# Differential attention: the transposition of the probabilities one slot later, from a buffer pair of their own

## Chip, cores and metric

One NeuronCore of a Trainium2 chip runs the whole program. The metric is the device time of one execution in microseconds (us). In this text PE is TensorE (the matmul engine), DVE is VectorE, ACT is ScalarE, SP is the queue that starts most of the loads. The engines run their own lists of instructions in order and meet through semaphores.

## The reference, cut to what matters

A trunk of two layers is applied to two request groups that share the weights: P (512 tokens) and S (256 tokens), model width 1024. Layer 0 mixes with a state-space model and gated linear attention, layer 1 with differential attention; each layer goes on with cross-attention over 256 memory tokens and a squared-ReLU MLP of width 4096. The part that is changed is this, for 8 heads, blocks of 128 queries, and all keys of the group:

```python
s = jnp.einsum('bqhzd,bkhzd->bzhqk', qblk, k) + bias[None, None]   # z: two maps per head
p = jax.nn.softmax(s, axis=-1)
attn = p[:, 0] - lam * p[:, 1]
return jnp.einsum('bhqk,bkhe->bqhe', attn, v)
# then, over the 128 values of each head: rms_norm(o, sub_norm) * (1 - lambda_init)
```

Computations are in float32. A projection is split in three products (high part of the weight by high part of the input, high by low, low by high).

## The kernel before

The tail of the kernel (`trunk_tail`) is one list of **slots** that is written out ahead of the run. A slot holds at most one weight **tile** (one 128-column stripe of a projection: 24 matmuls of 128x128 by 256 columns for group S, by 512 columns for group P, L1365 to L1378) and some **steps** of other work. `tile` takes the next steps from the front of `queue` (L1122); `drain` puts what is left of the queue in slots without a tile (L1133). Every engine walks the same list of slots and issues its part of each. SP loads the 512 KB of a tile in the order of the tiles.

For each tile ACT rounds the weights to the high part (`high`, L1348, for the tile three slots on) and DVE subtracts to get the low part (`low`, L1353, for the tile two slots on). An MLP "up" tile is closed by three ACT instructions (L1579 to L1581) and one of DVE (L1689); a "res" tile (down projection, output projection) by one of DVE (L1679).

Differential attention is done in items, one per head and block of 128 queries: 16 items for S, 32 for P (`Diff`). It is laid over the MLP tiles of the other group: the items of S over tiles of P, the items of P over tiles of S (L1248 to L1252 and L1271 to L1276). `diff_steps` makes a step for each slot t, and in slot t the engines do, in this order:

- PE: the scores of item t (L1482, banks 3 and 4, which wait for `neg` of item t-1), then the tile, then the transposes of the probabilities of item t-1 (L1495, bank 5, which wait for `prob`), then the product with the values of item t-2 (L1506), and, once per head, a sum of squares of the head that ended with item t-3 (L1513).
- DVE: `low`; the biased scores and their maximum of item t (L1802, then `neg`, L1808); the probabilities of item t-1 (L1778 to L1781: reciprocal, scale, lambda, combination; it signals `prob`); when item t-4 was a head's last, the norm of that head (L1656 to L1658, L1786); the close of the tile; L1815 for the norm. In the text "norm slot" is a slot that holds this norm, one in four for P.
- ACT: the exponentials of item t-1 (L1628), `high`, the close of an "up" tile, the copy of the transposed probabilities (L1639, signals `trc`), and its parts of the norm (L1643, L1525, L1526, L1649).

The scores with bias are written to `scb`, a pair of buffers by parity of the item, each with a half for each of the two maps. The exponentials are made in place, and so is the combination: L1781 writes the difference of the two maps over the first half, and L1495 reads it there. So L1802 of item t, which writes the same buffer again, waits for the transposes of item t-2 (L1800).

`vtmp` is a pair of 512-column buffers that the memory stage uses to bring the values out (L1709, stored by SP at L1328, signalled by `vout`); nothing else used it.

After the P items come the eight "res" tiles of the output projection (`dout`), then tiles of the S MLP (`mS.run(8)`, L1279) over which the norm of the new residual is applied in seven steps (`norm_steps(nP, FINE)`: statistic, then the eight stripes by L1728, L1596, L1735), then the query projection `q1`, whose first tile needs all eight stripes.

Of the kernel before, what the change touches and what calls it, by code (L numbers as in the profile page):

```python
# [13 lines left out]
ALU = mybir.AluOpType  # L14
# [3 lines left out]
P = 128  # L18
# [105 lines left out]
def build(nc, params, x_in, mem_in, wt_in, wglu_in, wgate_in, bc_in, tab_in, u_dram, y_dram, k_dram, v_dram, qk_dram, vog_dram,  # L124
          lr_dram, out):
    ctx = ExitStack()
    with ctx:
# [754 lines left out]
        def trunk_tail(mem, ymem):  # L882
# [267 lines left out]
            def diff_steps(d, qkv):  # L1150
                return [[("diff", d, qkv, t)] for t in range(d.n + 4)]

# [96 lines left out]
            later([], *diff_steps(dS, qkv))  # L1249
            mP.run(20)  # L1250
            later([("kvload", "S", 1, dS)])
# [3 lines left out]
            later([], *norm_steps(nS, PAIRS))  # L1255
            mP.run(7)
            q = Product("q", "S", WT["q1"], nS.ready)
# [14 lines left out]
            later([], *diff_steps(dP, qkv))  # L1272
            mS.run(37)
            nP = Norm("P", "cross1")
# [3 lines left out]
            later([], *norm_steps(nP, FINE))  # L1278
            mS.run(8)  # L1279
            qp = Product("q", "P", WT["q1"], nP.ready)  # L1280
# [205 lines left out]
            def pe_diff(pe, a, qkv_, t):  # L1486
                g, z = a.g, gs[a.g]
                nk = BL[g]
                if 0 <= t - 1 < a.n:
                    q_ = a.b + t - 1  # L1490
                    pe.wait_ge(prob.sem, q_ + 1)
                    if q_ >= 1:
                        pe.wait_ge(trc.sem, q_)
                    for j in range(nk):
                        last = nc.tensor.transpose(ps[:, 5, j * P:(j + 1) * P], scb[g][:, q_ % 2, 0, j * P:(j + 1) * P], ident)  # L1495
                    last.then_inc(tr.sem, 1)
                if 0 <= t - 2 < a.n:
                    q_ = a.b + t - 2
                    h, b = a.item(t - 2)
                    pe.wait_ge(trc.sem, q_ + 1)  # L1500
                    if t == 2:
                        pe.wait_ge(z["vcp"].sem, qkv_.vcp + KT)
                    if b == 0 and h >= 2:
                        pe.wait_ge(z["an"].sem, a.an + h - 1)
                    for j in range(nk):
                        last = nc.tensor.matmul(ps[:, 6 + h % 2, b * P:(b + 1) * P], dv[g][:, j, h * P:(h + 1) * P],  # L1506
                                                at[:, q_ % 2, j * P:(j + 1) * P], start=(j == 0), stop=(j == nk - 1))
                    last.then_inc(outd.sem, 1)
                if a.last(t - 3):
                    h = (t - 3) // BL[g]  # L1510
                    pe_bank(pe, (z["snew"].sem, a.stats[h].new))
                    pe.wait_ge(z["sqd"].sem, a.sq + h + 1)
                    nc.tensor.matmul(ps[:, 2, 0:N[g]], ones, ring[g][:, 0, :], start=True, stop=True).then_inc(z["ssum"].sem, 1)  # L1513
# [118 lines left out]
            def act_diff_copy(a, d_, t):  # L1632
                g, z = d_.g, gs[d_.g]
                if 0 <= t - 1 < d_.n:
                    q_ = d_.b + t - 1
                    a.wait_ge(tr.sem, q_ + 1)
                    if q_ >= 2:
                        a.wait_ge(outd.sem, q_ - 1)
                    nc.scalar.activation(at[:, q_ % 2, 0:N[g]], ps[:, 5, 0:N[g]], ACT.Copy).then_inc(trc.sem, 1)  # L1639
                if d_.last(t - 2):  # L1640
                    h = (t - 2) // BL[g]
                    a.wait_ge(outd.sem, d_.b + t - 1)
                    nc.scalar.activation(ring[g][:, 0, :], ps[:, 6 + h % 2, 0:N[g]], ACT.Square).then_inc(z["sqd"].sem, 1)  # L1643
                if d_.last(t - 3):
                    act_stat(a, d_.stats[(t - 3) // BL[g]])
                if d_.last(t - 4):
                    h = (t - 4) // BL[g]
                    a.wait_ge(z["an"].sem, d_.an + h + 1)
                    nc.scalar.activation(in_h[g][:, h, :], ring[g][:, 1, :], ACT.Copy).then_inc(z["ah"].sem, 1)  # L1649
# [122 lines left out]
            def dve_diff_prob(v, d_, t):  # L1772
                g, z = d_.g, gs[d_.g]
                if 0 <= t - 1 < d_.n:
# [5 lines left out]
                    dve_chain(nc.vector.tensor_tensor(s_[:, 7:8], s_[:, 7:8], lam[:, 5:6], ALU.mult))  # L1780
                    nc.vector.scalar_tensor_tensor(e_[:, 0, :], e_[:, 1, :], s_[:, 7:8], e_[:, 0, :], ALU.mult, ALU.add)\  # L1781
                        .then_inc(prob.sem, 1)
                if d_.last(t - 4):
                    h = (t - 4) // BL[g]
                    dve_stat(v, d_.stats[h])
                    nc.vector.scalar_tensor_tensor(ring[g][:, 1, :], ps[:, 6 + h % 2, 0:N[g]], gains[:, 1:2], y[g][:, :], ALU.mult, ALU.mult)\  # L1786
                        .then_inc(z["an"].sem, 1)

            def dve_diff_max(v, d_, t):
# [4 lines left out]
                if t < d_.n:  # L1794
# [4 lines left out]
                    if t >= 2:  # L1799
                        v.wait_ge(tr.sem, q_ - 1)  # L1800
                    for zz in range(2):
# [8 lines left out]
            def dve_diff_out(v, d_, t):  # L1810
                g, z = d_.g, gs[d_.g]
                if d_.last(t - 4):
                    h = (t - 4) // BL[g]
                    v.wait_ge(z["ah"].sem, d_.ah + h + 1)
# [563 lines left out]
```

## Time and profile before

| | |
|---|---|
| time, median of 3 runs | 2616.64 us (2608.69 to 2617.38) |
| profiled execution, its own time | 2618.24 us |
| its span, first to last instruction | 2616.5 us |
| PE busy | 2466.5 us (94%) |
| PE weight loads | 2088.8 us (80%) |
| DVE busy | 1533.7 us (59%) |
| ACT busy | 1149.9 us (44%) |
| mean granted TensorE clock | 0.978 |
| chain that ended last | PE 75%, DVE 9%, ACT 4% of the span |

Busy is the time in which an engine executed. Idle time stands in the rows in brackets or after a bar, with the instruction that ended it. The granted clock is the share of TensorE's full clock of 2.4 GHz that was let through in the stretch; 0.50 is 1.2 GHz.

### The profile page before, as it was taken

How to read it: one execution, taken by the hardware profiler on the slowest of the kernel's cores; microseconds unless marked ns; L12 is line 12 of the kernel's file. 1: busy time of each engine (PE TensorE's matmuls, PEld its weight loads, DVE VectorE, ACT ScalarE, POOL GpSimd, SP SyncE). 2: the span in 40 equal slices, each digit the busy share in tenths (PEclk: the TensorE clock that was granted, in tenths of full speed). 3: DMA queues.
4: the chain of work that ended last, by engine and by line, in shares of the span. 5: the costliest groups of instructions: out<-in, count | busy, mean ns of one | idle time of the engine just before them, and what ended most of it. 6: DMA issues, size and time to landing. Idle time of an engine off the chain costs nothing.

```text
span 2616.5 us, 35158 instructions
## 1 busy us (share of the span) xinstructions
PE 2466.5 (94%) x14102; PEld 2088.8 (80%) x14102; DVE 1533.7 (59%) x2587; ACT 1149.9 (44%) x2003; POOL 0.2 (0%) x4
## 2 busy tenths in 40 slices
PE   8988699899998899999999999999899999999999
PEld 4877576678887799899778888777677888888887
DVE  8998656657646655565565446656776635633332
ACT  4331335345433545554554344545565444433322
POOL 0000000000000000000000000000000000000000
PEclk9999799999999999999999999999999999999999
DMA  5333432245321365444224323223223432433332
GB/s 184 91 88 83 166 97 85 81 131 206 113 73 57 119 182 183 131 135 129 90 75 150 114 79 121 74 88 97 74 81 121 121 93 85 143 98 97 97 97 89
DMA packets 109666, 289.24 MB, mean 111 GB/s; under 512 B 18912, under 2 KB 41568, under 8 KB 108224
## 3 DMA queue, kind: packets, MB, share of 16 engines
q1 hardware_dynamic: 101392, 261.36, 32.5%
q10 hardware_dynamic: 8112, 25.63, 3.0%
q8 instruction: 113, 1.85, 0.3%
q14 instruction: 49, 0.40, 0.0%
HBM read 265.35 MB, written 19.50 MB: 109 GB/s over the span
## 4 chain that ended last, share of the span: by engine, by line
PE 75%; DVE 9%; ACT 4%; issue 1%; ACTq 0%; DVEq 0%
PE ps L1376 64%; PE ps L1439 2%; PE ps L1464 2%; DVE wlo L1353 1%; PE ps L1506 1%; PE ps L1482 1%; PE ps L1495 1%; DVE ps L1657 1%; DVE ps L1656 1%; PE ps L1408 1%; DVE yP L1658 1%; PE ps L1883 1%; ACT yP L1525 1%; DVE region_S L1781 1%; ACT whi L1348 1%
## 5 line engine op out<-in xcount | busy, mean ns | idle before, releaser
L1376 PE MATMUL ps<-in_hP,whi 128*128 128x512 f32 x1344 | 546.5, 407 | 4.4 <-DVE wlo L1353 2.8
L1353 DVE TENSOR_TENSOR wlo<-wraw,whi 128x1024 fp32r<-128x1024 f32 x432 | 524.7, 1218 | 36.8 <-ACT whi L1348 36.5
L1348 ACT ACTIVATE whi<-wraw 128x1024 fp32r<-128x1024 f32 x432 | 454.0, 1052 | 193.8 <-PE ps L1376 131.4
L1376 PE MATMUL ps<-in_hP,wlo 128*128 128x512 f32 x1344 | 527.4, 392 | 0.0
L1376 PE MATMUL ps<-in_lP,whi 128*128 128x512 f32 x1344 | 527.0, 392 | 0.0
L1376 PE MATMUL ps<-in_hS,whi 128*128 128x256 f32 x1088 | 321.1, 295 | 8.1 <-DVE hid_lS L1689 4.3
L1376 PE MATMUL ps<-in_lS,whi 128*128 128x256 f32 x1088 | 310.1, 285 | 0.0
L1376 PE MATMUL ps<-in_hS,wlo 128*128 128x256 f32 x1088 | 309.8, 285 | 0.0
L1376 PEld LDWEIGHTS ps<-in_hP,whi 128*128 128x128 f32 x1344 | 255.2, 190 | 67.3 <-issue 10.4
L1679 DVE TENSOR_TENSOR x<-ps,x 128x256 f32<-128x256 f32 (+1 forms) x192 | 107.0, 557 | 333.8 <-PE ps L1376 332.7
L1376 PEld LDWEIGHTS ps<-in_lP,whi 128*128 128x128 f32 x1344 | 255.2, 190 | 56.4 <-issue 5.3
L1376 PEld LDWEIGHTS ps<-in_hP,wlo 128*128 128x128 f32 x1344 | 254.5, 189 | 54.9
L1376 PEld LDWEIGHTS ps<-in_hS,whi 128*128 128x128 f32 x1088 | 211.0, 194 | 24.6 <-issue 18.9
L1376 PEld LDWEIGHTS ps<-in_lS,whi 128*128 128x128 f32 x1088 | 211.1, 194 | 2.4 <-issue 1.4
L1376 PEld LDWEIGHTS ps<-in_hS,wlo 128*128 128x128 f32 x1088 | 210.8, 194 | 0.0
L1376 PE MATMUL ps<-hid_hP,whi 128*128 128x512 f32 x512 | 202.0, 395 | 0.0
L1376 PE MATMUL ps<-hid_lP,whi 128*128 128x512 f32 x512 | 199.3, 389 | 0.0
L1376 PE MATMUL ps<-hid_hP,wlo 128*128 128x512 f32 x512 | 199.3, 389 | 0.0
L1689 DVE TENSOR_TENSOR hid_lP<-ps,hid_hP 128x512 fp32r<-128x512 f32 x64 | 44.3, 692 | 234.6 <-ACT hid_hP L1581 234.6
L1579 ACT ACTIVATE ps<-ps 128x512 f32<-128x512 f32 (+1 forms) x128 | 60.8, 475 | 251.7 <-PE ps L1376 251.7
L1376 PE MATMUL ps<-hid_hS,whi 128*128 128x256 f32 x512 | 148.6, 290 | 6.3 <-DVE hid_lS L1689 4.1
L1376 PE MATMUL ps<-hid_lS,whi 128*128 128x256 f32 x512 | 145.7, 285 | 0.0
(466 smaller groups left out, 3680.5 us busy)
## 6 DMA issues: line engine op xcount, KB each, us to landing
wraw<-wt SPq DMA_DIRECT2D x432, 512.0 KB, 3.5
wraw<-wt ACTq DMA_DIRECT2D x17, 512.0 KB, 4.2
k_scratch<-region_P SPq DMA_DIRECT2D x16, 256.0 KB, 2.9
v_scratch<-vtmp SPq DMA_DIRECT2D x32, 128.0 KB, 2.9
x<-x_in SPq DMA_DIRECT2D x4, 768.0 KB, 7.1
mix_u<-x SPq DMA_DIRECT2D x32, 64.0 KB, 3.3
mix_mem<-mem_in ACTq DMA_DIRECT2D x4, 512.0 KB, 6.4
x<-x_in ACTq DMA_DIRECT2D x1, 2048.0 KB, 12.9
```

The source lines that it names most:

```text
L1348: nc.scalar.activation(whi[:, n % NHI, :, :], wraw[:, ws(n), :, :], ACT.Copy).then_inc(wh.sem, 1)
L1353: nc.vector.tensor_tensor(wlo[:, ws(n), :, :], wraw[:, ws(n), :, :], whi[:, n % NHI, :, :].bitcast(F32), ALU.subtract).then_inc(wr.sem, 1)
L1376: last = nc.tensor.matmul(ps[:, m % 2, 0:N[prod.g]], w_[:, k, :], x_[:, k, :], start=(k == 0 and j == 0), stop=(k == KT - 1 and j == 2))
L1408: nc.tensor.matmul(ps[:, 2, 0:s.n], s.mat, ring[g][:, i % 2, :], start=True, stop=True).then_inc(z["ssum"].sem, 1)
L1439: last = nc.tensor.matmul(ps[:, 3 + q_ % 2, b * 256:(b + 1) * 256], qx[g][:, 2 * h + j, lo:lo + P], km[g][:, 2 * h + j, :], start=(j == 0) ...
L1464: last = nc.tensor.matmul(ps[:, 7, j * 256:(j + 1) * 256], vm[g][:, kt, (2 * h + j) * P:(2 * h + j + 1) * P], at[:, q_ % 2, kt * 256:(kt + ...
L1482: last = nc.tensor.matmul(ps[:, 3 + zz, 0:N[g]], dq[g][rows, h, b * P:(b + 1) * P], dk[g][rows, h, :], start=True, stop=True)
L1495: last = nc.tensor.transpose(ps[:, 5, j * P:(j + 1) * P], scb[g][:, q_ % 2, 0, j * P:(j + 1) * P], ident)
L1506: last = nc.tensor.matmul(ps[:, 6 + h % 2, b * P:(b + 1) * P], dv[g][:, j, h * P:(h + 1) * P], at[:, q_ % 2, j * P:(j + 1) * P], start=(j ...
L1579: act_chain(nc.scalar.activation(acc_ps, acc_ps, ACT.Relu))
L1679: nc.vector.tensor_tensor(x[:, i, cols(g)], ps[:, b, 0:N[g]], x[:, i, cols(g)], ALU.add).then_inc(tf[b].sem, 1)
L1689: nc.vector.tensor_tensor(hid_l[g][:, i, :], ps[:, b, 0:N[g]], hid_h[g][:, i, :].bitcast(F32), ALU.subtract)\
```

## The change

The transposes of an item move one slot later, and everything behind them with it (product with the values, sum of squares, norm, copies): they run in slot t for item t-2, and `diff_steps` is one slot longer (n + 5 steps). L1781 writes its result to `vtmp` instead of over `scb`, and the transposes read it there. DVE waits ahead of L1781 until the transposes of the item two before have read the buffer; the wait of L1802 on `tr` becomes one on `prob`, DVE's own signal. In the first item of each group DVE waits once for the memory stage's last stores out of `vtmp`. One MLP tile more is laid over each group's items, and one fewer over the norm that follows the output projection: 21 and 6 instead of 20 and 7 for the items of S, 38 and 7 instead of 37 and 8 for those of P. The number and the kinds of instructions are the same.

```diff
--- before.py
+++ after.py
@@ -1148,7 +1148,7 @@
                 return [[("cross", a, t)] for t in range(a.n + 2)]
 
             def diff_steps(d, qkv):
-                return [[("diff", d, qkv, t)] for t in range(d.n + 4)]
+                return [[("diff", d, qkv, t)] for t in range(d.n + 5)]
 
             class Mlp:
 
@@ -1247,13 +1247,13 @@
                     mP.run(1)
             dS = Diff("S")
             later([], *diff_steps(dS, qkv))
-            mP.run(20)
+            mP.run(21)
             later([("kvload", "S", 1, dS)])
             drain()
             nS = Norm("S", "cross1")
             run(Product("res", "S", WT["dout"], dS.ready, norm=nS))
             later([], *norm_steps(nS, PAIRS))
-            mP.run(7)
+            mP.run(6)
             q = Product("q", "S", WT["q1"], nS.ready)
             run(q)
             a = Cross("S", 1)
@@ -1270,13 +1270,13 @@
             mS = Mlp("S", 1, nS, None)
             dP = Diff("P")
             later([], *diff_steps(dP, qkv))
-            mS.run(37)
+            mS.run(38)
             nP = Norm("P", "cross1")
             later([("kvload", "P", 1, dP)])
             drain()
             run(Product("res", "P", WT["dout"], dP.ready, norm=nP))
             later([], *norm_steps(nP, FINE))
-            mS.run(8)
+            mS.run(7)
             qp = Product("q", "P", WT["q1"], nP.ready)
             run(qp)
             ap_ = Cross("P", 1)
@@ -1486,19 +1486,19 @@
             def pe_diff(pe, a, qkv_, t):
                 g, z = a.g, gs[a.g]
                 nk = BL[g]
-                if 0 <= t - 1 < a.n:
-                    q_ = a.b + t - 1
+                if 0 <= t - 2 < a.n:
+                    q_ = a.b + t - 2
                     pe.wait_ge(prob.sem, q_ + 1)
                     if q_ >= 1:
                         pe.wait_ge(trc.sem, q_)
                     for j in range(nk):
-                        last = nc.tensor.transpose(ps[:, 5, j * P:(j + 1) * P], scb[g][:, q_ % 2, 0, j * P:(j + 1) * P], ident)
+                        last = nc.tensor.transpose(ps[:, 5, j * P:(j + 1) * P], vtmp[:, q_ % 2, j * P:(j + 1) * P], ident)
                     last.then_inc(tr.sem, 1)
-                if 0 <= t - 2 < a.n:
-                    q_ = a.b + t - 2
-                    h, b = a.item(t - 2)
+                if 0 <= t - 3 < a.n:
+                    q_ = a.b + t - 3
+                    h, b = a.item(t - 3)
                     pe.wait_ge(trc.sem, q_ + 1)
-                    if t == 2:
+                    if t == 3:
                         pe.wait_ge(z["vcp"].sem, qkv_.vcp + KT)
                     if b == 0 and h >= 2:
                         pe.wait_ge(z["an"].sem, a.an + h - 1)
@@ -1506,8 +1506,8 @@
                         last = nc.tensor.matmul(ps[:, 6 + h % 2, b * P:(b + 1) * P], dv[g][:, j, h * P:(h + 1) * P],
                                                 at[:, q_ % 2, j * P:(j + 1) * P], start=(j == 0), stop=(j == nk - 1))
                     last.then_inc(outd.sem, 1)
-                if a.last(t - 3):
-                    h = (t - 3) // BL[g]
+                if a.last(t - 4):
+                    h = (t - 4) // BL[g]
                     pe_bank(pe, (z["snew"].sem, a.stats[h].new))
                     pe.wait_ge(z["sqd"].sem, a.sq + h + 1)
                     nc.tensor.matmul(ps[:, 2, 0:N[g]], ones, ring[g][:, 0, :], start=True, stop=True).then_inc(z["ssum"].sem, 1)
@@ -1631,20 +1631,20 @@
 
             def act_diff_copy(a, d_, t):
                 g, z = d_.g, gs[d_.g]
-                if 0 <= t - 1 < d_.n:
-                    q_ = d_.b + t - 1
+                if 0 <= t - 2 < d_.n:
+                    q_ = d_.b + t - 2
                     a.wait_ge(tr.sem, q_ + 1)
                     if q_ >= 2:
                         a.wait_ge(outd.sem, q_ - 1)
                     nc.scalar.activation(at[:, q_ % 2, 0:N[g]], ps[:, 5, 0:N[g]], ACT.Copy).then_inc(trc.sem, 1)
-                if d_.last(t - 2):
-                    h = (t - 2) // BL[g]
-                    a.wait_ge(outd.sem, d_.b + t - 1)
+                if d_.last(t - 3):
+                    h = (t - 3) // BL[g]
+                    a.wait_ge(outd.sem, d_.b + t - 2)
                     nc.scalar.activation(ring[g][:, 0, :], ps[:, 6 + h % 2, 0:N[g]], ACT.Square).then_inc(z["sqd"].sem, 1)
-                if d_.last(t - 3):
-                    act_stat(a, d_.stats[(t - 3) // BL[g]])
                 if d_.last(t - 4):
-                    h = (t - 4) // BL[g]
+                    act_stat(a, d_.stats[(t - 4) // BL[g]])
+                if d_.last(t - 5):
+                    h = (t - 5) // BL[g]
                     a.wait_ge(z["an"].sem, d_.an + h + 1)
                     nc.scalar.activation(in_h[g][:, h, :], ring[g][:, 1, :], ACT.Copy).then_inc(z["ah"].sem, 1)
 
@@ -1778,10 +1778,14 @@
                     dve_chain(nc.vector.reciprocal(s_[:, 6:8], s_[:, 4:6]))
                     nc.vector.tensor_scalar(e_[:, 0, :], e_[:, 0, :], s_[:, 6:7], None, ALU.mult)
                     dve_chain(nc.vector.tensor_tensor(s_[:, 7:8], s_[:, 7:8], lam[:, 5:6], ALU.mult))
-                    nc.vector.scalar_tensor_tensor(e_[:, 0, :], e_[:, 1, :], s_[:, 7:8], e_[:, 0, :], ALU.mult, ALU.add)\
+                    if t == 1:
+                        for i in range(2):
+                            v.wait_ge(vout[i].sem, 32 * KT)
+                    v.wait_ge(tr.sem, max(d_.b, q_ - 1))
+                    nc.vector.scalar_tensor_tensor(vtmp[:, q_ % 2, 0:N[g]], e_[:, 1, :], s_[:, 7:8], e_[:, 0, :], ALU.mult, ALU.add)\
                         .then_inc(prob.sem, 1)
-                if d_.last(t - 4):
-                    h = (t - 4) // BL[g]
+                if d_.last(t - 5):
+                    h = (t - 5) // BL[g]
                     dve_stat(v, d_.stats[h])
                     nc.vector.scalar_tensor_tensor(ring[g][:, 1, :], ps[:, 6 + h % 2, 0:N[g]], gains[:, 1:2], y[g][:, :], ALU.mult, ALU.mult)\
                         .then_inc(z["an"].sem, 1)
@@ -1797,7 +1801,7 @@
                     off = 384 - P * b
                     v.wait_ge(sc_done.sem, q_ + 1)
                     if t >= 2:
-                        v.wait_ge(tr.sem, q_ - 1)
+                        v.wait_ge(prob.sem, q_ - 1)
                     for zz in range(2):
                         nc.vector.tensor_tensor_reduce(
                             out=scb[g][:, q_ % 2, zz, :], in0=ps[:, 3 + zz, 0:keys], in1=dist[:, off:off + keys],
@@ -1809,8 +1813,8 @@
 
             def dve_diff_out(v, d_, t):
                 g, z = d_.g, gs[d_.g]
-                if d_.last(t - 4):
-                    h = (t - 4) // BL[g]
+                if d_.last(t - 5):
+                    h = (t - 5) // BL[g]
                     v.wait_ge(z["ah"].sem, d_.ah + h + 1)
                     nc.vector.tensor_tensor(in_l[g][:, h, :], ring[g][:, 1, :], in_h[g][:, h, :].bitcast(F32), ALU.subtract)\
                         .then_inc(z["ar"].sem, 1)
```

## Rows read from the trace of the kernel before

**Rows 1.** Windows of the S items and the P items: start:end, us, busy (x), clock, DMA.
```profile
1259.15:1390.17 131.02, 131.02 (x632) 103.16 (x632) 79.05 (x217) 69.06 (x161) 0.00 (x0) 1.00 0.26 77
1782.70:2007.00 224.30, 202.37 (x1369) 162.65 (x1368) 168.77 (x394) 134.86 (x282) 0.00 (x0) 0.97 0.26 83
```

**Rows 2.** Waits, 1782 to 2006 us: waiter <- releaser: us in total, times, longest.
```profile
PE ps L1495 <- DVE region_S L1781: 21.3, 15, 2.6
```

**Rows 3.** Timeline of PE, first transposes of the P items, then after two norm slots.
```profile
1792.66 0.66 PE L1495 MATMUL ps<-par,region_S 128*128 128x128 f32 x4 [1.21 <-DVE region_S L1781]
...
1827.08 0.66 PE L1495 MATMUL ps<-par,region_S 128*128 128x128 f32 x4 [0.30 <-DVE region_S L1781]
...
1835.34 0.66 PE L1495 MATMUL ps<-par,region_S 128*128 128x128 f32 x4 [2.59 <-DVE region_S L1781]
...
1997.10 0.86 PE L1495 MATMUL ps<-par,region_S 128*128 128x128 f32 x4 [2.41 <-DVE region_S L1781]
```

**Rows 4.** Chain of waits from 1835 us: start, us, what.
```profile
1835.34 0.66 PE ps L1495 x4
1835.99 0.89 PE ps L1506 x8
1836.88 1.06 PE ps L1482 x4
1837.94 3.06 PE ps L1376 x24
```

**Rows 5.** Timeline of DVE through a norm slot and the next, 1826 to 1836 us.
```profile
1826.94 0.69 DVE L1656 SCALAR_TENSOR_TENSOR ps<-ps,yP 128x512 f32<-128x512 f32 x1
...
1829.80 0.42 DVE L1679 TENSOR_TENSOR x<-ps,x 128x256 f32<-128x256 f32 x1
...
1831.19 1.22 DVE L1353 TENSOR_TENSOR wlo<-wraw,whi 128x1024 fp32r<-128x1024 f32 x1
...
1833.67 0.17 DVE L1808 TENSOR_SCALAR st<-st 128x2 f32<-128x2 f32 x1
...
1835.19 0.42 DVE L1679 TENSOR_TENSOR x<-ps,x 128x256 f32<-128x256 f32 x1
1835.53 1.22 DVE L1353 TENSOR_TENSOR wlo<-wraw,whi 128x1024 fp32r<-128x1024 f32 x1
```

**Rows 6.** Windows: one head at full clock, then the first and last half-clock stretch.
```profile
1861.78:1888.21 26.43, 23.54 (x162) 18.57 (x162) 20.90 (x50) 16.39 (x34) 0.00 (x0) 1.00 0.26 79
1888.21:1891.20 2.99, 2.99 (x14) 2.76 (x16) 1.42 (x2) 1.83 (x5) 0.00 (x0) 0.50 0.09 36
...
1997.10:2000.10 3.00, 3.00 (x15) 3.00 (x16) 1.56 (x2) 1.61 (x3) 0.00 (x0) 0.55 0.18 68
```

**Rows 7.** Chain of waits: the head of a half-clock slot.
```profile
1942.77 1.12 PE ps L1495 x4
1943.88 1.71 PE ps L1506 x8
1945.59 1.38 PE ps L1482 x4
```

**Rows 8.** Line L1781: duration ns min/median/max, first and last start us.
```profile
L1781 DVE SCALAR_TENSOR_TENSOR region_S<-region_S,st x32: 750/752/753, 1791.8 to 1996.3; 128x512 f32<-128x512 f32 x32
```

**Rows 9.** Timeline of PE over the P norm: the S tiles, then query tile 0.
```profile
2068.53 0.38 PE L1376 MATMUL ps<-hid_hS,whi 128*128 128x256 f32 x1 [2.41 <-DVE hid_lS L1689]
...
2081.99 0.40 PE L1376 MATMUL ps<-in_hP,whi 128*128 128x512 f32 x1
```

**Rows 10.** Window behind that wait of PE.
```profile
2068.50:2072.00 3.50, 3.47 (x18) 3.47 (x19) 3.50 (x6) 1.68 (x3) 0.00 (x0) 0.58 0.45 145
```

**Rows 11.** Chain of waits, a tile of group P that follows another.
```profile
1378.76 5.49 PE ps L1376 x24
```

**Rows 12.** Timeline of DVE over the P norm, first wait and last stripes.
```profile
2068.05 0.42 DVE L1689 TENSOR_TENSOR hid_lS<-ps,hid_hS 128x256 fp32r<-128x256 f32 x1 [0.99 <-ACT hid_hS L1581]
...
2083.22 1.29 DVE L1735 TENSOR_TENSOR in_lP<-ringP,in_hP 128x512 fp32r<-128x512 f32 x2
```

## The prediction

> **What bounds the kernel now.** The windows come first, because the change touches two stretches only. While the items of S are worked off, PE is busy for all of its 131.02 us at granted clock 1.00; while those of P are, it is busy 202.37 of 224.30 us at 0.97 [rows 1]. So there is nothing to win over S, and about 22 us of idle PE over P. The waits name their cause: 21.3 us in 15 waits of the transposes (L1495) for the probabilities (L1781) [rows 2]. The timeline sorts them: one of 1.21 us at the first item, seven of about 0.3 us, and seven of 2.4 to 2.6 us, in pairs, one pair for each of seven heads [rows 3]. The eighth head's norm falls in a slot without items, and nobody waits.
>
> Why in pairs follows from DVE's list. In the chain an ordinary slot of PE is transposes 0.66, values 0.89, scores 1.06, tile 3.06, together 5.67 us [rows 4]; with the sum of squares once per head a head is 23.54 us of work and lasted 26.43 us [rows 6]. DVE goes from one `low` to the next in 4.34 us (1831.19 to 1835.53) where it waits for nobody. A norm slot has 2.86 us more (1826.94 to 1829.80) and 1.05 us more around L1815 (1.39 from L1679 to `low`, against 0.34) [rows 5], together 8.25 us. DVE needs 4 x 4.34 + 2.86 + 1.05 = 21.27 us per head, less than PE's 23.54. DVE is therefore not the bound. Its one long slot is, because PE wants a result made in the same slot: 2.59 us behind the norm, and 0.3 us in the norm slot itself, where the exponentials stand behind ACT's statistic.
>
> **The change, part by part.** *Waits of the transposes.* In slot t they now read item t-2, whose `prob` was signalled in DVE's slot t-1. I count from T, the end of the tile in the norm slot, 1826.78 (1827.08 less its wait of 0.30) [rows 3]. DVE's late result reached PE at 1835.34, T + 8.56 [rows 3]. It is now wanted by the transposes two slots on, at T + 11.34. Margin 2.8 us, so the waits go, all 15: -21.3 us, the first item's too, since its transposes now come a whole slot later. Bounds: none of it if the wait only moves, all 21.3 if nothing follows.
>
> *What is late next.* The scores of t+2 need `neg` of t+1 (L1808). It starts at 1833.67 and takes 0.17 us, T + 7.06 [rows 5]; with some 0.05 us to arrive, T + 7.1. PE, no longer held, gets there at 5.67 + 0.66 + 0.89 = T + 7.22. It fits by 0.1 us. DVE is then still 2.8 us behind the end of PE's tile, and wins back 1.33 us a slot (5.67 - 4.34): caught up before the next norm. I take 0, with bounds 0 and the whole 2.59 us at seven heads. Low parts are made two slots ahead and `td`, `tf` and `trc` look back at least a slot; within 2.8 us of lag none of them comes due.
>
> *Half clock.* Four of the seven long waits are followed by a stretch in which TensorE was granted about half its clock, 0.50 in the first and 0.55 in the last [rows 6]. Such a slot opens with 1.12, 1.71 and 1.38 us in place of 0.66, 0.89 and 1.06 [rows 7, 4], 1.60 us lost; the four together, read the same way, 6.0 us. There are none over S, where PE never idles (1.00) [rows 1]. With the waits gone I count the four gone: -6.0 us, bounds 0 and 6.0. The Trainium skill, "TensorE: Matmul & The Clock Gate", section "HAM oscillation — how this bites in real kernels", has the same mechanism: idling between bursts of matmuls puts the clock back to half, and the work behind starts slow. By that rule the 6.0 us go with the idle time. But here three waits of the same length cost no clock, so the trace ties the two only loosely, and without the rule one would leave the 6.0 us in, a result that stands among the rivals.
>
> *Buffer pair.* L1781 has the same shape as before, 750 to 753 ns over all 32 [rows 8], and only its target differs: 0. Its new wait on `tr` is for the transposes of item t-3 in slot t, which PE issued in slot t-1. L1802, earlier in the same DVE slot, already waits for scores that PE issues behind them. It can't be the last. The waits on `vout` concern stores of the memory stage, hundreds of us back. A wait instruction more per item lies in DVE's 1.33 us of slack. Behind it are queued the norm, the close of the tile (L1679, L1689) and `low`; PE's tile two slots on waits for those. The wait moved off L1802 becomes one on DVE's own signal of a slot earlier: 0.
>
> *Stages one slot longer.* The added slot carries a tile that was run later anyway, so PE's work is the same. The loads keep their number, SP's queue changes nothing but that one S tile or P tile comes ahead of the eight `dout` tiles; POOL has no part. Over S, ends and waits stay as they are (131.02 of 131.02 us busy). The norm behind S's `dout` keeps five P tiles of 5.49 us [rows 11] over five short steps and stays covered: 0.
>
> *The norm behind P's `dout`.* It has seven S tiles for cover, not eight, and here DVE sets the pace. Today PE waits 2.41 us for L1689 [rows 9], because the first down-projection tile falls right on the statistic; behind it the clock is 0.58 [rows 10]. With one tile fewer that tile comes a slot later, its inputs are closed before the statistic, and that wait goes. DVE, which waited 0.99 us there, ends the last stripes about 1 us earlier than 2083.22 + 1.29 = 2084.5 [rows 12], at 2083.5. Query tile 0 can't end before that plus an eighth of 5.49 us: 2084.2. Today it starts at 2081.99 [rows 9] and ends about 2087.5, but has one S tile of some 3 us (3.06 behind scores [rows 4]) more behind it. So 2084.2 against 2084.5: -0.3 us. New gaps of 2 to 3 us inside query tile 0 can cost the clock once, +1.5. I take +1, bounds -0.5 and +4 (the lost cover, and 1.5).
>
> **Sum**, against the profiled execution of 2618.24 us (span 2616.5 and 1.7 around it): -21.3 - 6.0 + 1.0 = -26.3, so 2591.9 us. The median shown is 1.6 us under the profiled execution: 2590.3, and I say **2590**.
>
> **Rivals.** *A. The clock stays low in places.* The waits go and the 6.0 us don't, since it is not settled that the waits cause them: 2596. For it: three like waits without it. Against it: S at 1.00.
>
> *B. The wait moves on to the scores.* If DVE's `neg` is later than in the trace, L1482 waits for L1808 where L1495 waited for L1781. The 0.1 us in hand are worked out from single starts, and each us that L1808 comes late costs one at seven heads. At worst the seven long waits and the clock behind them stay and only 1.21 + 2.1 us go, with +1 for the norm: 2614. For it: the small margin. Against it: the two waits look at different points of DVE's slot; L1808 lies 1.5 us ahead of L1781's signal, while PE arrives 1.55 us later than it did at the transposes.
>
> *C. DVE sets the pace, slower than before.* Over P, with PE no longer pausing, DVE has no slot in which to catch up if its instructions are longer for running beside PE and ACT without pause. It decides when a head of DVE exceeds the 26.96 us that a head now lasts on average ((1997.10 - 1835.34) / 6 [rows 3]), that is when DVE's 21.27 us grow by over 5.7. If the four instructions L1778 to L1781, about 1.6 us of the slot, took double, it would be 21.27 + 6.4 = 27.7, 0.7 us more for each of eight heads and the 1 us of the norm: 2624. Against it: 750 to 753 ns, with and without PE busy beside it.
>
> *D. The change does nothing where it counts.* The transposes still wait, now for `trc` of the item before or for the buffer: 2616. The copy into `at` is one slot old then, which speaks against it.
>
> **How the numbers follow.** Forecast 0.76, A 0.08, B 0.07, C 0.05, D 0.04. About 0.5% (13 us) is what a measurement of this kernel tells from no change. The forecast and A are faster by more than that, and a partial B, with up to 10 us kept, too: 0.86. The rest of B, and D: 0.09. C: 0.05. The range reaches down to 2582, because the three executions shown spread from 8 us under their median to 1 above and the median after may fall likewise, and up to 2606 for A and the part of B in between; the likeliest case alone has 2583 to 2597.
>
> **What would show it.** Right: no wait of L1495 for L1781 over the P items, heads of about 23.6 us, nine tenths of DVE's time filled, granted clock 0.99 or more there, and that stretch about 24 us shorter in all, with one S tile of 3.06 us more in it. L1689 no longer holds PE over the norm, and L1735 does inside query tile 0. S's stretch is one P slot longer, with PE as busy. Wrong: L1482 waiting for L1808 at the slot behind each norm (B), low clock without idle time (A), DVE without gaps and PE with them (C).

## The result, and the profile after

| | before | after |
|---|---|---|
| median, runs beside each other | 2612.66 us (2607.89 to 2617.38, 4 runs) | 2584.68 us (2576.72 to 2587.69, 4 runs) |
| profiled execution | 2618.24 us | 2576.72 us |
| granted TensorE clock | 0.978 | 0.984 |

The ratio is 0.9875, with a 95% interval of 0.9856 to 0.9894: 1.25% less time, 28 to 38 us of 2612.66. The two medians of the table are 28.0 us apart, at the small end of that; executions of one kernel spread over some 10 us, and four of each leave a median loose. A second measurement, on another chip, gave 0.9875 (0.9847 to 0.9903), with medians 33.7 us apart. The forecast took off 26.3 us, 1.0%, a ratio of 0.990. The direction and the cause were right, and the size was too small by a little more than the interval allows.

The two profiles are 41.6 us of span apart, more than the change is worth. To see why, the program is cut where stages begin. First the windows of before: up to the S items, the S items (to the last sum of squares), up to the P items, the P items, the norm behind them with the query projection. Columns as in [rows 1].

```profile
0.00:1259.10 1259.10, 1150.20 (x7182) 989.66 (x7182) 815.42 (x1340) 547.87 (x945) 0.20 (x4) 0.96 0.40 123
1259.10:1390.20 131.10, 131.10 (x632) 103.23 (x632) 79.05 (x217) 69.06 (x162) 0.00 (x0) 1.00 0.26 77
1390.20:1782.70 392.50, 381.89 (x1944) 321.30 (x1942) 210.52 (x301) 170.00 (x272) 0.00 (x0) 0.99 0.34 105
1782.70:2007.10 224.40, 202.47 (x1369) 162.65 (x1368) 168.77 (x394) 134.96 (x282) 0.00 (x0) 0.97 0.26 83
2007.10:2133.30 126.20, 122.67 (x659) 106.32 (x657) 62.62 (x80) 51.90 (x78) 0.00 (x0) 0.99 0.40 126
```

The same stages of the kernel after:

```profile
0.00:1251.20 1251.20, 1143.68 (x7180) 984.45 (x7180) 815.35 (x1340) 548.63 (x945) 0.20 (x4) 0.97 0.40 124
1251.20:1388.00 136.80, 136.80 (x658) 107.85 (x657) 80.99 (x219) 71.85 (x166) 0.00 (x0) 1.00 0.25 78
1388.00:1773.60 385.60, 374.97 (x1920) 315.26 (x1918) 208.71 (x299) 168.02 (x268) 0.00 (x0) 1.00 0.34 106
1773.60:1968.80 195.20, 192.83 (x1392) 159.75 (x1392) 168.14 (x396) 136.38 (x286) 0.00 (x0) 1.00 0.32 98
1968.80:2091.80 123.00, 118.64 (x636) 101.96 (x634) 60.94 (x78) 50.00 (x74) 0.00 (x0) 1.00 0.40 126
```

The first stage is 7.9 us shorter, though no edit touches it; that is not the change. The four others were 874.2 us together and are 840.6, 33.6 us less, which is near what the ratio says (1.25% of 2612.66 is 32.7). What comes behind them takes 483.2 us before and 483.1 after. The moved tile shows in the counts of PE (23 of its 24 matmuls were recorded): the P items have one S tile more and the stage behind them one fewer. So over the P items the gain is 29.2 us and that tile of 3.06 us, 32.3 us.

Now the waits over the P items of the kernel after (waiter <- releaser: us in total, times, longest):

```profile
PEld ps L1482 <- DVE st L1812: 3.7, 7, 0.5
PE ps L1482 <- DVE st L1812: 2.4, 7, 0.3
```

No wait of L1495 is left, against 15 [rows 2]. A small one has come at the scores, six times behind a norm slot and once at the first item, where it was before. Then the chain of an ordinary slot of the kernel after, from its transposes to the next:

```profile
1791.01 0.44 PE ps L1495 x4
1791.45 0.89 PE ps L1506 x8
1792.34 1.06 PE ps L1482 x4
1793.40 3.06 PE ps L1376 x24
1796.46 0.44 PE ps L1495 x4
```

Three of its four pieces are those of [rows 4]. The transposes take 0.44 us where they took 0.66, and that I had not foreseen. It could have been seen in two rows of the kernel before, the first from the waits over the P items and the second from the timeline of an ordinary slot's weight loads (PEld; the probabilities are what is loaded):

```profile
PEld ps L1495 <- DVE region_S L1781: 28.1, 32, 2.8
```

```profile
1841.00 0.42 PEld L1495 LDWEIGHTS ps<-par,region_S 128*128 128x128 f32 x4 [0.20 <-DVE region_S L1781]
```

The matmul row of the same wait has 15 entries, the weight load's row has 32, one per item. In this ordinary slot the load waited 0.2 us for L1781 and began at 1841.00, just as the tile of [rows 4] ended (1837.94 + 3.06). In the matmul row the transposes follow the tile without idle time, so it shows no wait, and the lateness stands inside their 0.66 us.

The margin at the scores looks like this in the kernel after, DVE's norm slot first and then PE:

```profile
1842.40 0.69 DVE L1656 SCALAR_TENSOR_TENSOR ps<-ps,yP 128x512 f32<-128x512 f32 x1
...
1846.04 0.69 DVE L1819 TENSOR_TENSOR in_lP<-ringP,in_hP 128x512 fp32r<-128x512 f32 x1 [0.37 <-ACT in_hP L1649]
1846.65 1.22 DVE L1353 TENSOR_TENSOR wlo<-wraw,whi 128x1024 fp32r<-128x1024 f32 x1
...
1849.12 0.17 DVE L1812 TENSOR_SCALAR st<-st 128x2 f32<-128x2 f32 x1
```

```profile
1849.34 1.13 PE L1482 MATMUL ps<-region_P 64*128 64x512 f32 x4 [0.34 <-DVE st L1812]
```

DVE does what it did: from L1656 to the maximum 6.72 us, 6.73 in [rows 5]. PE waits 0.34 us for it.

### The profile page after: what moved, and what is told of

Its sections match the earlier page's. It is cut to its first block, busy times and chain, and to the rows that moved or that the text cites. A ratio compares the mean times of both kernels' runs of the same rounds, so it can differ in the third digit from the quotient of the medians.

```text
span 2574.9 us, 35208 instructions
## 1 busy us (share of the span) xinstructions
PE 2445.1 (95%) x14102; PEld 2074.9 (81%) x14102; DVE 1531.4 (59%) x2587; ACT 1151.0 (45%) x2003; POOL 0.2 (0%) x4
## 4 chain that ended last, share of the span: by engine, by line
PE 76%; DVE 8%; ACT 3%; issue 1%; ACTq 0%; DVEq 0%
PE ps L1376 65%; PE ps L1439 2%; PE ps L1464 2%; DVE wlo L1353 1%; PE ps L1482 1%; PE ps L1506 1%; DVE ps L1657 1%; DVE ringP L1728 1%; DVE ps L1656 1%; PE ps L1408 1%; DVE yP L1658 1%; ACT yP L1525 1%; PE ps L1887 1%; ACT whi L1348 0%; PE ps L1495 0%
## 5 line engine op out<-in xcount | busy, mean ns | idle before, releaser
L1679 DVE TENSOR_TENSOR x<-ps,x 128x256 f32<-128x256 f32 (+1 forms) x192 | 107.0, 557 | 334.3 <-PE ps L1376 333.9
L1689 DVE TENSOR_TENSOR hid_lP<-ps,hid_hP 128x512 fp32r<-128x512 f32 x64 | 44.3, 692 | 231.9 <-ACT hid_hP L1581 231.9
```

The costliest lines, as they stand in the source:

```text
L1679: nc.vector.tensor_tensor(x[:, i, cols(g)], ps[:, b, 0:N[g]], x[:, i, cols(g)], ALU.add).then_inc(tf[b].sem, 1)
L1689: nc.vector.tensor_tensor(hid_l[g][:, i, :], ps[:, b, 0:N[g]], hid_h[g][:, i, :].bitcast(F32), ALU.subtract)\
```

## The experiments

**Which group has the gain.** The change for group S alone, with the P items and their tiles as before:

```diff
-return [[("diff", d, qkv, t)] for t in range(d.n + 5)]
+return [[("diff", d, qkv, t)] for t in range(d.n + 4 + LATE[d.g])]   # LATE = {"S": 1, "P": 0}
-mS.run(38) ... mS.run(7)
+mS.run(37) ... mS.run(8)
# in the steps of PE, ACT and DVE: t - 1 - LATE[g] for t - 2, and so on; vtmp only where LATE[g] is 1
```

> The change is made for the items of group S alone; those of P, and the tiles laid over them, stay as before. My theory (all the gain is in the P items, where PE waited for the probabilities): no change, within 3 us of before, and over the P items the same 15 waits of L1495 for L1781, about 21 us, with transposes that take 0.66 us. Rival (the pair of buffers or the later slot help in themselves, by calmer engines or fewer conflicts): the S items give their share too, 16 of 48 items of a gain of some 33 us, so about 11 us faster than before.

Measured: 0.9987 (0.9968 to 1.0006). Waits over its P items (L1498 and L1789 are L1495 and L1781 of the kernel before):

```profile
PEld ps L1498 <- DVE region_S L1789: 28.0, 32, 2.8
PE ps L1498 <- DVE region_S L1789: 21.2, 15, 2.6
```

No change that can be told, and no third of the gain. The stages show 1.3 us of it: S items and the stage behind them are 522.3 us, against 523.6 before. The kernel after has the same (522.4). These 1.3 us are one stretch of low clock behind the wait of 2.6 us in the first tile of the S output projection. Its window is shown first for the kernel before, then for the kernel after:

```profile
1395.71:1400.00 4.29, 4.29 (x23) 4.29 (x24) 2.55 (x3) 2.42 (x3) 0.00 (x0) 0.61 0.87 345
```

```profile
1393.45:1398.00 4.55, 4.55 (x38) 4.55 (x39) 3.56 (x5) 2.84 (x4) 0.00 (x0) 1.00 0.94 351
```

The wait ahead is 2.6 us in both. It is not a matter of single executions: of the thirteen profiles of this text, the five of kernels without the whole change over S (before, the pair of buffers alone, the later slot alone, the dependence taken away, L1815 later) have the stretch there, and the eight of kernels with it don't, at waits of 2.1 to 3.3 us. Why the clock held in the eight is left open; the length of the wait is not what tells them apart.

**The pair of buffers alone**, transposes in the same slot as before:

```diff
-transpose(..., scb[g][:, q_ % 2, 0, j * P:(j + 1) * P], ident)      # still item t - 1
+transpose(..., vtmp[:, q_ % 2, j * P:(j + 1) * P], ident)
-nc.vector.scalar_tensor_tensor(e_[:, 0, :], e_[:, 1, :], ...)
+v.wait_ge(tr.sem, max(d_.b, q_ - 1))      # and, in the first item, the wait on vout
+nc.vector.scalar_tensor_tensor(vtmp[:, q_ % 2, 0:N[g]], e_[:, 1, :], ...)
-v.wait_ge(tr.sem, q_ - 1)      # ahead of the biased scores
+v.wait_ge(prob.sem, q_ - 1)
```

> Only the pair of buffers: L1781 writes to it, and the transposes read it in the same slot as before. The kernel with the whole change shows transposes of 0.44 us in the chain where the kernel before has 0.66, in each of the 32 P items, 7 us in all that my prediction did not count. Theory 1 (the 0.22 us are a wait too: the weights of the transposes are loaded only once L1781 is done, 0.2 us late in every ordinary slot): still 0.66 us, the 15 waits stay, the time is that of before within 3 us. Rival (the 0.22 us belong to the place read: the region that DVE and ACT write at the same time): 0.44 us, and about 7 us faster than before.

Measured: 0.9993 (0.9978 to 1.0009). Its waits over the P items, and a transposition from its chain:

```profile
PEld ps L1495 <- DVE vtmp L1785: 28.0, 32, 2.8
PE ps L1495 <- DVE vtmp L1785: 21.3, 15, 2.6
```

```profile
1838.99 0.66 PE ps L1495 x4
```

The place read plays no part: with the pair of buffers and the wait the transposes still take 0.66 us. That the 0.22 us are a wait is shown by the run without the dependence, below. (Its P items took 221.5 us, 2.9 less than before, with the same waits and two stretches of low clock for four.)

**The later slot alone**, in place over the scores:

```diff
-v.wait_ge(tr.sem, max(d_.b, q_ - 1))      # and, in the first item, the wait on vout
-nc.vector.scalar_tensor_tensor(vtmp[:, q_ % 2, 0:N[g]], e_[:, 1, :], ...)
+nc.vector.scalar_tensor_tensor(e_[:, 0, :], e_[:, 1, :], ...)
-v.wait_ge(prob.sem, q_ - 1)      # ahead of the biased scores
+v.wait_ge(tr.sem, q_ - 1)
```

> Only the later slot: the transposes run one slot later, but read the combination over the scores as before, so the biased scores of item t (L1806 in the changed kernel's numbering) must wait for the transposes of item t-2, which now come after the tile of slot t. Theory 1 (DVE's list is what is late, and the pair of buffers is what frees it): DVE starts the biased scores about 0.5 us after the end of the tile, the next scores wait for them, an ordinary slot takes about 6.1 us instead of 5.67 and the norm slot about 8.3; a head some 27 us, as long as before (26.96) or longer. Time within 10 us of before, and PE waits for the maximum (L1812) instead of for L1781. Rival (the later slot is what brings the gain, the buffers are only needed to be safe): 25 us or more faster than before.

Measured: 1.0045 (1.0031 to 1.006), 12 us slower than before. Waits over the P items:

```profile
PEld ps L1482 <- DVE st L1808: 40.9, 30, 2.9
PE ps L1482 <- DVE st L1808: 31.5, 24, 2.7
DVE region_S L1802 <- PE ps L1495: 52.1, 24, 4.8
```

Now DVE waits for the transposes before it writes the biased scores (third row), and PE waits for the maximum in turn. The P items take 231.7 us, 36.5 more than with both parts, with three stretches of low clock behind six waits of 2.7 us. The S items take 145.5 us against 136.8. The rival is out. I had put it within 10 us of before and not counted S: there PE's idle time, none before, is 7.8 us. Neither part does anything good alone.

**The dependence taken away, the order kept:**

```diff
-pe.wait_ge(prob.sem, q_ + 1)
-transpose(..., scb[g][:, q_ % 2, 0, j * P:(j + 1) * P], ident)      # still item t - 1
+transpose(..., vtmp[:, q_ % 2, j * P:(j + 1) * P], ident)
-v.wait_ge(tr.sem, q_ - 1)      # ahead of the biased scores
+v.wait_ge(prob.sem, q_ - 1)
```

> The kernel before, but the transposes read the pair of buffers that nothing writes in this stage, and don't wait for the probabilities: the attention of layer 1 is then computed from other numbers, and no slot is moved. It takes the dependence away and leaves the order. Theory 1 (every part of the gain is time in which PE waited for L1781, half clock behind such waits included): over the P items transposes of 0.44 us, heads of about 23.0 to 23.3 us as in the changed kernel, no half clock there, 30 to 34 us less over that stage than before; the wait of 2.41 us for L1689 over the norm behind them stays. Time 28 to 36 us under before. Rival A (half clock is not from the waits): 6 us less gain, stretches of 0.5 remain. Rival B (the gain needs the moved tiles): 2 to 5 us less gain.

Measured: 0.9869 (0.9854 to 0.9883), 34 us under before. The window of its P items and a transposition of its chain:

```profile
1783.60:1975.90 192.30, 189.93 (x1368) 156.71 (x1368) 166.86 (x394) 134.37 (x282) 0.00 (x0) 1.00 0.31 97
```

```profile
1802.34 0.44 PE ps L1494 x4
```

These are 192.3 us with one S tile fewer than in the kernel after; with its 3.06 us that is 195.4, against 195.2. The transposes take 0.44 us in the very slot where they took 0.66, so the 0.22 us were a wait. All that the change brings over the P items is time that PE spent waiting for L1781, with what hangs on such waits. There is no low clock over the P items any more, and the small wait for the maximum is here too (2.4 us).

**The moved S tile put back:**

```diff
-mS.run(38) ... mS.run(7)
+mS.run(37) ... mS.run(8)
```

> The changed kernel with the S tiles laid as before: 37 over the P items and 8 over the norm behind the output projection. The last slot of the P items, with the norm of the eighth head, then has no tile over it. Theory 1 (the moved tile is what hides the added slot): PE waits there for the norm's chain at the last stripe of the output projection's first tile: after the last sum, ACT's close of the tile and statistic and DVE's norm, about 6.3 us, against 5.5 us of that first tile for its first seven eighths, 4.8: about 1.5 us idle. Over the norm it is as before, with PE waiting 2.4 us for L1689 and half clock behind it. Together 0.3 to 3 us slower than the changed kernel. Rival (an uncovered slot costs a whole slot's work of DVE and ACT): 6 us or more slower than the changed kernel.

Measured: 0.9878 (0.9849 to 0.9906) of before. P items and the stage behind them, the uncovered slot included, are 195.2 + 123.7 = 318.9 us, against 318.2 in the kernel after: 0.7 us. In PE's timeline, the wait in the uncovered slot:

```profile
1987.39 0.50 PE L1376 MATMUL ps<-in_hP,whi 128*128 128x512 f32 x1 [1.24 <-DVE in_lP L1819]
```

The wait for L1689 over the norm is back with 2.4 us, but no low clock behind it. The added slot costs next to nothing even without a tile over it: the output projection's own first tile runs meanwhile, and PE waits 1.24 us in it.

**The low part of the normed head (L1819) a slot later**, in the kernel after:

```diff
-for t in range(d.n + 5)
+for t in range(d.n + 6)
 def dve_diff_out(v, d_, t):
-    if d_.last(t - 5): h = (t - 5) // BL[g]
+    if d_.last(t - 6): h = (t - 6) // BL[g]
```

> The changed kernel with the low part of a head's normed output (L1819) one slot later, so that DVE's norm slot is 1.05 us shorter. The changed kernel has a new wait of 0.34 us of the scores (L1482) for the maximum (L1812) behind each of seven norm slots, 2.4 us in all. Theory 1 (DVE's norm slot is too long by that much): the seven waits go, a head takes about 22.7 us instead of 23.08, 2.4 us less over the P items. Rival (PE arrives earlier and waits for something else, such as ACT's copy of the transposed items or a low part of a tile): heads stay at 23.08.

Measured: 0.9855 (0.9825 to 0.9884). The P items take 192.7 us, 2.5 less, and of the waits for the maximum only the one at the first item is left:

```profile
PE ps L1482 <- DVE st L1812: 0.3, 1, 0.3
```

That one is in the kernel before as well, so the change had brought six waits of 0.34 us, not seven: behind the norm of the seventh head there are no scores left two slots on.

It was measured again beside the kernel after.

> The changed kernel once more, beside the one with L1819 a slot later, on the same chip: the P items at 195 us, the time 0.9855 to 0.989 of before. The stretch ahead of the S items, which no edit touches, took 1251.2 us in two of the profiles and 1258 to 1263 in the others; I expect one or the other here too, and it says how much of a difference between two profiles is not the change.

> The changed kernel with L1819 a slot later, measured once more beside the changed kernel: P items at 192.7 us against 195.2, no difference elsewhere, so 2.5 us (0.1%) faster than the changed kernel, at the limit of what the intervals can tell. Rival (it is given back over the next stages): P items shorter and the sum of the stages from the S items on the same as in the changed kernel.

Measured: 0.9875 (0.9847 to 0.9903) for the kernel after, 0.987 (0.9843 to 0.9897) with L1819 later. The P items are 195.3 and 192.7 us, as in the first pair. From the S items on, the stages make 842.0 against 838.1 us; 1.5 of these 3.9 us lie in the norm behind the P items, where one profile has a stretch of low clock and the other has none. The profiles show the 2.5 us over the P items twice; the times can't tell the two kernels apart. The stretch ahead of the S items took 1260.0 and 1261.9 us.

**The same edit in the kernel before**, L1815 a slot later:

```diff
-for t in range(d.n + 4)
+for t in range(d.n + 5)
-    if d_.last(t - 4): h = (t - 4) // BL[g]      # dve_diff_out
+    if d_.last(t - 5): h = (t - 5) // BL[g]
```

> The kernel before with the low part of a head's normed output (L1815) one slot later: its seven waits of 2.4 to 2.6 us for L1781 become 1.05 us shorter, about 1.5 us. Theory 1 (each us of DVE's norm slot stands in PE's time): 7.4 us less over the P items. For the half clock: if it comes only behind waits of over about 2 us, the four stretches go too, 6 us more, 13 us under before in all; if it has nothing to do with the length of the wait, about four remain and it is 7 us.

Measured: 0.9964 (0.995 to 0.9977), 9 us. Over the P items:

```profile
1783.90:1997.10 213.20, 197.93 (x1370) 158.64 (x1369) 168.19 (x394) 135.00 (x282) 0.00 (x0) 0.99 0.29 87
```

```profile
PE ps L1495 <- DVE region_S L1781: 14.6, 15, 2.1
```

The waits are 6.7 us shorter and the stage 11.2. The rest is low clock: one stretch, where before had four.

**DVE's load against its longest slot.** The same number of added instructions, once spread, one per item:

```diff
+dve_chain(nc.vector.tensor_scalar(vtmp[:, q_ % 2, 0:N[g]], e_[:, 0, :], 1.0, None, ALU.mult))   # ahead of L1785
```

> The changed kernel with one more instruction of DVE per item, of 512 columns for P and 256 for S, ahead of L1785, which writes over its result; about 0.5 us with what lies around it. It prices the nearness of DVE's bound. DVE's list per head of P grows from about 21.3 us by 4 x 0.45 to 0.55 to 23.1 to 23.5 us, against 22.7 us of PE. Theory 1 (DVE has 1.4 us of slack per head and no more): DVE becomes the bound over the P items, a head takes 23.2 to 23.8 us instead of 23.08, 1 to 6 us slower than the changed kernel, and PE waits for L1812. Rival (DVE is far from the bound, as its busy share over the whole span of 59% suggests): no change. Rival (each instruction added is paid in full): 32 x 0.5 = 16 us slower.

and once all in the norm slot:

```diff
+for _ in range(BL[g]):
+    dve_chain(nc.vector.tensor_scalar(y[g][:, :], y[g][:, :], 1.0, None, ALU.mult))   # behind dve_stat
```

> The changed kernel with as many added DVE instructions per head as in the run with one more per item (four of 512 columns for P, two of 256 for S, here a multiplication of the norm's factor by 1), but all in the norm slot. It tells the load of DVE from the length of its longest slot. Theory 1 (what counts is when the slot behind the norm gives its maximum, since four ordinary slots have slack each): each added instruction takes 0.46 us of that slot, so the seven waits of the scores for the maximum grow from 0.34 by 1.84 to about 2.2 us, 15 us in all; the P items take 13 us more than in the changed kernel (195.2), about 208, against 198.0 for the same load spread over the slots. Half clock may come back behind such waits, 1.6 us each. Rival (DVE's load per head is what counts, 23.1 us against PE's 22.7): the same 198 us as with the load spread.

Measured: 0.9883 (0.9859 to 0.9907) spread, 0.996 (0.9948 to 0.9972) in one slot. First the P items with the work spread, then with it in one slot, DVE busy for 181 us in both:

```profile
1782.00:1980.00 198.00, 192.88 (x1392) 159.72 (x1392) 181.32 (x428) 136.35 (x286) 0.00 (x0) 1.00 0.32 96
```

```profile
1784.90:1998.50 213.60, 199.04 (x1392) 165.29 (x1392) 180.85 (x424) 136.28 (x286) 0.00 (x0) 0.97 0.28 89
```

The waits of PE over the P items, spread (first row) and in one slot (the two others), and the window behind one wait of the latter:

```profile
PE ps L1482 <- DVE st L1813: 5.1, 7, 0.8
PE ps L1482 <- DVE st L1814: 13.4, 7, 2.2
PE ps L1376 <- DVE hid_lS L1689: 1.1, 1, 1.1
```

```profile
1917.18:1921.50 4.32, 4.32 (x19) 3.56 (x20) 4.21 (x12) 2.93 (x7) 0.00 (x0) 0.64 0.00 0
```

Spread over the slots, 13 us of added DVE work cost 2.8 us, and these too come from the norm slot: six waits have grown from 0.34 to 0.80 us, by the one added instruction that falls there (5.1 less 2.4 is 2.7 us). The three others of each head cost nothing. In one slot the same work costs 18.4 us. Of these 11.0 are waits for the maximum (13.4 less 2.4), 1.1 is a new wait for L1689 in the last slots, and the rest, 6.3, goes with four stretches of low clock that have come back at another place and another line. I had 13 us for it and left the clock open.

## Why the prediction was right in its cause and short in its size

*The waits of the transposes*, -21.3 us: right, all 15 gone; the run without the dependence shows that nothing else in the stage is part of the gain.

*An ordinary slot of 5.67 us without a wait*: this is the step that failed. I took 0.66 us as the duration of the transposes, and it held 0.22 us of wait, so the sum had nothing for a gain in the ordinary slots. The row of the weight loads gives it: 28.1 - 21.3 = 6.8 us over the P items. I had read only the matmul row. The buffer pair alone keeps the 0.66, the dependence taken away gives 0.44, so it is a wait for L1781. A head was to take about 23.6 us and takes 23.08 (1849.34 to 1872.42, from one wait of L1482 to the next).

*What is late next*, 0 with 0.1 us in hand: wrong, and by the same 0.22 us. From T to the scores of t+2 PE passes two groups of transposes, each 0.22 us shorter than I had it: 7.22 - 0.44 = 6.78, and `neg` comes at T + 7.11. That makes 0.33 us of wait, measured 0.34, at six heads, +2.1 us. With L1819 a slot later the six are gone, which shows that the norm slot's length makes them. Rival B was this wait at full size; it came at an eighth of that.

*Half clock*, -6.0 us: the four stretches are gone, and none is left over the P items. The amount was one draw. With the very same 15 waits the profile before had four stretches, that of the S-only kernel five and that of the buffers alone two, some 8 and 3 us (a stretch shows in the products with the values, 1.9 us in place of 1.06). The tie to the waits, which I called loose, is shown over the P items by taking them away and bringing them back: no stretch in the seven profiles in which no wait of PE there is longer than 0.8 us; one stretch with a wait of 2.1 us (and none behind six of 1.5); three behind six waits of 2.7 with the later slot alone; four behind six waits of 2.2 with the norm slot made longer. That is the side of the Trainium skill's rule ("TensorE: Matmul & The Clock Gate", "HAM oscillation — how this bites in real kernels") and against rival A. What decides whether one such wait costs the clock is not settled by these runs, and it is not its length alone: at the S output projection the same wait of 2.6 us does in one kernel and doesn't in another, and behind the query projection a stretch follows a wait of 1.1 us for L1712 in four of the thirteen profiles. So the -6.0 was right in its cause, and that it fitted the profile before is no more than that profile's own count of four.

*Buffer pair and its waits*, 0: right, neither `tr` nor `vout` ends a wait of DVE there, and nobody waits for L1785.

*The stages of S*, 0: 1.3 us of gain, by one stretch of low clock; the wait ahead of it did not change. Not foreseen, and its cause is open.

*The norm behind the P output projection*, +1: measured 126.2 to 123.0 us with an S tile (2.88 us) fewer, -0.3, which is the sum as I worked it out (-0.3) without the half-clock stretch that I added. The second profile of the kernel after has that stretch (124.4 us, +1.1). The wait for L1689 is gone, and in its place stands one for the last stripes, as forecast; one of 1.07 us for L1679 has come too, which I had not counted:

```profile
2044.40 0.50 PE L1376 MATMUL ps<-in_hP,whi 128*128 128x512 f32 x1 [2.18 <-DVE in_lP L1735]
```

The sum with the two corrected terms: -21.3 - 6.0 - 6.8 + 2.1 = -32.0 over the P items, measured 224.4 to 195.2 with an S tile of 3.06 more, -32.3. With -1.2 for S (523.6 to 522.4), -0.3 for the norm, and 0.2 because the moved tile takes 3.06 us where it is now and took 2.88 where it was, that is the -33.6 of the stages.

Rival C (DVE sets the pace): DVE is busy for 168 of 195 us, and 13 us more of it, spread, cost 2.8, all of it by the norm slot. It is near the bound but not at it. Rival D (the transposes still wait, for something else) is out, since no wait of L1495 is left.

## What to carry to other kernels

When one engine waits for another's result in the same pipeline slot, look at the longest slot of the one that makes it, not at its load: here DVE with 59% of the span busy cost PE 21 us, and the same 13 us of work cost 2.8 us spread and 18.4 in one slot. A step later in the pipeline needs its own buffer, or the wait only changes its place: each part alone gave nothing or a loss.

Read the weight-load rows beside the matmul rows before calling a slot free of waits, and treat a margin of 0.1 us built from such a slot as none.

## What was not expected of the hardware

The stretch ahead of the S items, the same in all kernels, took 1251.2 and 1251.3 us in two profiles (the kernel after, and the pair of buffers alone) and 1259.1 to 1263.2 in the eleven others: two single profiles can differ by 12 us, 0.5% of the span, without any change. Most of it is one place. The same stretch of work in the profile of before and in that of the kernel after:

```profile
381.00:437.00 56.00, 50.44 (x199) 36.91 (x200) 25.91 (x46) 23.80 (x45) 0.00 (x0) 0.88 0.30 102
380.00:430.00 50.00, 44.43 (x200) 32.56 (x201) 26.20 (x47) 24.11 (x46) 0.00 (x0) 1.00 0.36 115
```

PE's first wait in it is 2.1 us in both; behind it the clock falls to half in the eleven (granted clock 0.86 from 380 to 430 us in each) and stays full in the two (1.00). Comparing stage by stage took it out.
